# Norms, constants and the last blocks taken by halves in a three-block kernel on one core

## What is computed

```python
def third_block(x, c, ...):
    mod = jax.nn.silu(c) @ w_ada + b_ada
    shift1, scale1, gate1, shift2, scale2, gate2 = jnp.split(mod, 6, axis=-1)
    h = rms_norm_3(x, norm1_pre) * (1.0 + scale1) + shift1
    z = h @ w_in
    y_a = spatial_gating(z[..., : 2 * D_A], ...)
    y_b = multiscale_pool(z[..., 2 * D_A:], ...)
    mix = jnp.concatenate([y_a, y_b], axis=-1) @ w_out
    x = x + gate1 * rms_norm_3(mix, norm1_post)
    h = rms_norm_3(x, norm2_pre) * (1.0 + scale2) + shift2
    f = jnp.square(jax.nn.relu(h @ w_fc1)) @ w_fc2
    x = x + gate2 * rms_norm_3(f, norm2_post)
    return x
```

## Time and profile before

| | |
|---|---|
| median of 3 runs | 3709.75 us (3709.17 to 3716.92) |
| profiled execution | 3709.14 us, span 3707.4 us |
| mean granted TensorE clock | 0.965 |
| busy: PE | 3542.8 us (96%) |
| busy: DVE, ACT, POOL | 43%, 27%, 34% |
| DMA | 239.79 MB, mean 65 GB/s |

### The profile page before, as it was taken

One profiled execution on the slowest core, in us unless ns is written; L12 is line 12 of the kernel. 1 busy time (PEld: TensorE's weight loads), 2 busy tenths in 40 slices (PEclk: granted clock), 3 DMA queues, 4 the chain that ended last, 5 costly groups with the idle time before them and its releaser, 6 DMA issues.

```text
span 3707.4 us, 39394 instructions
## 1 busy us (share of the span) xinstructions
PE 3542.8 (96%) x17066; PEld 2843.6 (77%) x17066; DVE 1600.2 (43%) x1611; ACT 999.8 (27%) x1422; POOL 1253.5 (34%) x628
## 2 busy tenths in 40 slices
PE   8999999999999999989999999999998889999997
PEld 6888888888888787545787777877877678888885
DVE  4643443433335383546545445444535341222224
ACT  5423221111113211545332212212322332222221
POOL 3113245444445131002223334434524343333332
PEclk9999999999999999959999999999999899999998
DMA  2112222222223121100211222221311111111113
GB/s 104 46 57 80 91 71 86 89 90 80 83 83 114 35 69 37 39 3 1 74 46 51 87 84 63 90 86 62 95 36 34 63 54 46 49 49 49 49 49 114
DMA packets 87416, 239.79 MB, mean 65 GB/s; under 512 B 13110, under 2 KB 20038, under 8 KB 87116
## 3 DMA queue, kind: packets, MB, share of 16 engines
q1 hardware_dynamic: 87244, 237.28, 19.8%
HBM read 219.27 MB, written 17.97 MB: 64 GB/s over the span
## 4 chain that ended last, share of the span: by engine, by line
PE 91%; DVE 5%; ACT 2%; POOL 1%; issue 0%; DMA 0%; SPq 0%; DVEq 0%; ACTq 0%
PE ps L570 27%; PE ps L571 27%; PE ps L573 26%; PE ps L877 1%; PE ps L907 1%; PE ps L927 1%; PE ps L942 1%; PE ps L705 1%; PE ps L625 1%; PE ps L989 1%; PE ps L973 1%; DVE T L1713 1%; DVE T L1738 0%; DVE P L2113 0%; DVE T L1716 0%
## 5 line engine op out<-in xcount | busy, mean ns | idle before, releaser
L2425 POOL TENSOR_TENSOR wlo<-raw,whi 128x1024 fp32r<-128x1024 f32 (+3 forms) x368 | 698.6, 1898 | 1713.6 <-ACT whi L1155 1713.2
L570 PE MATMUL ps<-HH,whi 128*128 128x512 f32 (+2 forms) x2816 | 1119.6, 398 | 46.8 <-DVE HL L1729 13.7
L571 PE MATMUL ps<-HL,whi 128*128 128x512 f32 (+2 forms) x2816 | 1106.7, 393 | 0.0
L573 PE MATMUL ps<-HH,wlo 128*128 128x512 f32 (+2 forms) x2816 | 874.8, 392 | 0.0
L1155 ACT ACTIVATE whi<-raw 128x1024 fp32r<-128x1024 f32 (+3 forms) x368 | 310.9, 845 | 1722.6 <-PE ps L573 1548.2
L570 PEld LDWEIGHTS ps<-HH,whi 128*128 128x128 f32 (+2 forms) x2816 | 531.7, 189 | 168.8 <-DVE HL L1729 18.3
L570 PE MATMUL ps<-GH,whi 128*128 128x512 f32 x1536 | 609.7, 397 | 15.7 <-POOL wlo L2425 12.5
L573 PEld LDWEIGHTS ps<-HH,wlo 128*128 128x128 f32 (+2 forms) x2816 | 530.6, 188 | 116.7 <-issue 0.6
L571 PEld LDWEIGHTS ps<-HL,whi 128*128 128x128 f32 (+2 forms) x2816 | 531.8, 189 | 112.9 <-issue 2.0
L571 PE MATMUL ps<-GL,whi 128*128 128x512 f32 x1536 | 601.6, 392 | 0.0
L573 PE MATMUL ps<-GH,wlo 128*128 128x512 f32 x1536 | 477.1, 392 | 0.0
(11 more groups left out here) (335 smaller groups left out, 2930.7 us busy)
## 6 DMA issues: line engine op xcount, KB each, us to landing
raw<-in_w_up SPq DMA_DIRECT2D x76, 512.0 KB, 3.4
raw<-in_w_in SPq DMA_DIRECT2D x70, 512.0 KB, 3.3
raw<-in_w_fc SPq DMA_DIRECT2D x64, 512.0 KB, 3.3
raw<-in_w_down SPq DMA_DIRECT2D x104, 256.0 KB, 2.7
raw<-in_w_ada SPq DMA_DIRECT2D x48, 512.0 KB, 3.4
raw<-in_w_fc SPq DMA_DIRECT2D x64, 256.0 KB, 2.7
X<-in_xT SPq DMA_DIRECT2D x16, 512.0 KB, 7.3
raw<-in_w_out SPq DMA_DIRECT2D x16, 512.0 KB, 3.3
```

Of the source, the lines that this page charges most:

```text
L570: e.matmul(o_[0:m, half(hf)], whi_[:, k, :], hi[k0 + k][:, half(hf)], start=first, stop=False)
L571: e.matmul(o_[0:m, half(hf)], whi_[:, k, :], lo[k0 + k][:, half(hf)], start=False, stop=False)
L573: i = e.matmul(o_[0:m, half(hf)], wlo_[:, k, :], hi[k0 + k][:, half(hf)], start=False, stop=last)
L2425: e.tensor_tensor(wlo_of(name), raw_of(name), whi_of(name).bitcast(F), SUB).then_inc(*po.inc("lo " + name))
```

## The change

Five parts:

1. **Spreads.** The spread of the norms n2, n3, nl, n4 and n5 goes into misc in the middle of a product, instead of into a PSUM buffer after it. ScalarE's copy to RT stands ahead of the next weight split. The conv norm's sums (nl) come one product later, its spread within the one after.
2. **Constants.** ADA_AT loses items 0, 1, 2 and gains 51, 63, 75. ROW_AT is redrawn. Before: every item from 3 to 61 except those that 4 divides. After: 2, 3, 4, 13, then in each group three of the four up items (14, 15, 16; 26, 27, 28; ...) and seven of the eight down items (19 to 25; 31 to 37; ...). Before the group's last hidden tile, ScalarE and GpSimd now split the next down products' weights.
3. **The mixer's end.** wo36 and wo37 are taken by halves of the tokens: both for the first half, then both for the second. Norm, mixn, x6, hh6, hl6 and squares go by halves.
4. **Three up products by blocks.** fa1_0, fa1_1 and fa1_2 go along together: for each half and block, the three matmuls of each. A third high-half buffer WX serves fa1_1.
5. **The tail.** fa2_7_6 and fa2_7_7 by halves; nf, xo, out and the output DMAs by halves; the gain is multiplied into X by ScalarE ahead.

```diff
-ADA_AT = sorted([0, 1, 2] + [n for n in range(4, 88) if (n - 4) % 12 in (0, 1, 2, 5, 7, 9)] + [15, 27, 39])
-ROW_AT = [n for n in range(3, 62) if n % 4]
+ADA_AT = sorted([n for n in range(4, 88) if (n - 4) % 12 in (0, 1, 2, 5, 7, 9)] + [15, 27, 39, 51, 63, 75])
+ROW_AT = [n for n in range(2, 62) if n < 5 or n == 13 or 14 <= n < 53 and (n - 14) % 12 < 3
+          or n >= 18 and (n - 18) % 12 in range(1, 8)]
...
         def tensor(e):
+            def halves(names, hi, lo, toks, nk, k0=0, between=None, along=False):
+                parts = []
+                for hf in range(2):
+                    order = [(n, k) for k in range(nk) for n in range(len(names))] if along else [(n, k) for n in range(len(names)) for k in range(nk)]
+                    for n, k in order:
+                        if n == len(parts):
+                            parts.append((take(names[n]),) + weights(names[n], nk))
+                            q.wait_ge(*po("lo " + names[n]))
+                        o_, whi_, wlo_ = parts[n]
+                        if between:
+                            between(names[n], hf, k)
+                        for tok in toks(k0 + k, hf):
+                            q.wait_ge(*tok)
+                        e.matmul(o_[:, half(hf)], whi_[:, k, :], hi[k0 + k][:, half(hf)], start=k == 0, stop=False)
+                        e.matmul(o_[:, half(hf)], whi_[:, k, :], lo[k0 + k][:, half(hf)], start=False, stop=False)
+                        i = e.matmul(o_[:, half(hf)], wlo_[:, k, :], hi[k0 + k][:, half(hf)], start=False, stop=k == nk - 1)
...
-            job("gv0", hhs, hls, h3, 8)
-            spread("n3 sp", two, dv("n3 r12"))
+            job("gv0", hhs, hls, h3, 8, between=lambda k: k == 6 and spread_misc("n3 sp", two, dv("n3 r12"), dv("n3 s2")))
...
-            job("zv1", hhs, hls, h5, 8)
-            spread("n5 sp", two, dv("n5 r12"))
+            job("zv1", hhs, hls, h5, 8, between=lambda k: k == 5 and spread_misc("n5 sp", two, dv("n5 r12"), dv("b43")))
...
-            sums("nm", dv("nm acc7"))
-            spread("nm sp", one, dv("nm r1"))
-            mlp("fa1_", "fa2_", [4] * 8, lambda k: [dv(f"hl6 {k}")], "nx", dv("nx acc7"), joint=True)
-            sums("nf", dv("nf acc7"))
-            spread("nf sp", one, dv("nf r1"))
+            def mix_norm(name, hf, k):
+                if (name, hf, k) == ("wo36", 1, 4):
+                    sums_half("nm", 0, 512, dv("nm acc7 h0"))
+                elif (name, hf, k) == ("wo37", 1, 1):
+                    spread_half("nm", 0, misc, dv("nm r1 h0"))
+            halves(["wo36", "wo37"], hhs, hls, lambda k, hf: [y3[k]], 8, between=mix_norm)
+            def next_norm(name, hf, k):
+                if (name, hf, k) == ("fa1_0", 0, 3):
+                    sums_half("nm", 1, 512, dv("nm acc7 h1"), ac("nm sd h0"))
+                elif (name, hf, k) == ("fa1_0", 0, 7):
+                    spread_half("nm", 1, misc, dv("nm r1 h1"))
+                elif (name, hf, k) == ("fa1_0", 1, 4):
+                    sums_half("nx", 0, 0, dv("nx acc7 h0"), dv("mixn 7 0"))
+            halves(["fa1_0", "fa1_1", "fa1_2"], hhs, hls, lambda k, hf: [dv(f"hl6 {k} {hf}")], 8, between=next_norm, along=True)
+            sums_half("nx", 1, 512, dv("nx acc7 h1"), dv("mixn 7 1"))
+            spread_half("nx", 0, misc, dv("nx r1 h0"))
+            spread_half("nx", 1, misc, dv("nx r1 h1"))
...
         def scalar(e):
+            mixed(6, 0)
+            mixed(7, 0)
+            root_half("nm", 0, 512)
+            mixed(6, 1)
+            behind("wo36")
+            highs(widx["fa1_1"])
+            for hf in range(2):
+                h = half(hf)
+                for k in range(8):
+                    high(f"hh6 {k} {hf}", X[:, k, h], HH[:, k, h], po(f"x6 {k} {hf}"), pe("wo37"), scale=gains[:, 16 + k:17 + k])
+                    if (k, hf) == (1, 0):
+                        mixed(7, 1)
+                        highs(widx["fa1_2"])
...
+            root_half("nx", 1, 512)
+            for hf in range(2):
+                q.wait_ge(*pe(f"nx sp{hf}"))
+                e.activation(RT[:, half(hf)], misc[:, half(hf)], ACT.Copy).then_inc(*ac.inc("nx rt" if hf else "nx rt0"))
...
         def gpsimd(e):
+                    if g and j == SIZES2[g] - 1:
+                        for j_ in range(3 if g == 1 else 1):
+                            behind(f"fdn{g - 1}_{j_}")
                     low(f"fuplo{m}", T[CT[m][1]][:], GH[:, sl, :], GL[:, sl, :], ac(f"fuphi{m}"))
```

More of the change, by code:

```diff
@@ L856, in tensor @@
                 for m in range(3):
-                    job(f"{name}{m}", hhs, hls, h3, 8)
+                    job(f"{name}{m}", hhs, hls, h3, 8, between=None if n != 15 else lambda k: k == 5 and spread_misc("nl sp", one, dv("nl r1")))
                     turn_now()
@@ L1073, in tensor @@
                         sums("n4", dv("n4 acc7"))
-                    job(f"fupb{m}", hhs, hls, lambda k: [dv(f"hl4 {k}")], 8)
-                    if m == 0:
-                        spread("n4 sp", one, dv("n4 r1"))
+                    job(f"fupb{m}", hhs, hls, lambda k: [dv(f"hl4 {k}")], 8,
+                        between=None if m else lambda k: k == 5 and spread_misc("n4 sp", one, dv("n4 r1")))
                 else:
@@ L1369, in mlp @@
                         f = 4 * g + j
+                        if f == 1 and norm:
+                            to_rt(norm, *rt_free)
                         behind(f"{up}{f}")
@@ L1687, in scalar @@
                     q.wait_ge(*po("y3l3"))
-                square("nm", m, ps[slot[f"wo3{m}"]][:], *([dv("uu3")] if m == 0 else []))
-                e.activation(MIX[:, m, :], ps[slot[f"wo3{m}"]][:], ACT.Copy, scale=gains[:, 8 + m:9 + m]).then_inc(*ac.inc(f"mix{m}", f"free wo3{m}"))
-            root("nm", 1024)
-            done = 0
-            for k in range(8):
-                high(f"hh6 {k}", X[:, k, :], HH[:, k, :], at_x6(k), pe("wo37"), scale=gains[:, 16 + k:17 + k])
-                if k in (0, 1, 2, 4, 6):
-                    square("nx", done, X[:, done, :], *([pe("nm sp")] if k == 0 else []))
-                    done += 1
```

300 lines of the change are left out of this document (201 added, 99 removed).

## The result

The changed kernel takes 3618.5 us in the median of four runs (3615.57 to 3619.77), against 3711.26 us before (3709.17 to 3716.92, four runs). The ratio is 0.9747, with a 95% interval from 0.973 to 0.9763: faster, by 92.8 us. The profiled execution has a span of 3616.3 us (before 3707.4), and its mean granted clock is 0.975 (before 0.965).

What follows compares the result with a forecast made beforehand. TensorE bounds the kernel, 91% of the span; the change can only remove standstill or low clock. Gains of 26, 33, 18 and 5 us sum to 82, giving 3627, median 3628 us; range 3603 to 3656, chance 0.83.

Steps and rivals of the forecast that it cites:

- Spreads inside products: Five norms' spreads moved into the middle of products: TensorE's gaps and clock dips there go; gain 26 us, bounds 0 to 26.
- the nine microseconds of the conv norm: Conv norm: the 4.81 us wait for its sums and a 4.2 us clock dip go, 9.0 us.
- Constants moved: Second MLP's constants moved, weights split earlier: 14.5 of 47.5 us stay; gain 33 us, bounds 10 and 47.5.
- the rival of a binding supply: Each of 28 down products with a constant waits 0.8 us, so that region gains 10 us: 3651; chance 0.13.
- The slower rival: The constants' reduction falls behind in each of 28 rows, slower from 3.7 us a row on: 3773; chance 0.03.
- The mixer's end: Last output products to the fourth up product, by halves: 53.6 us against 71.3; gain 18 us, bounds 0 and 30.
- The first block comes 1.4 us later: Mixer's end: HH may be written only when both last output products are through, delaying the first block 1.4 us.
- The third product's 3.8 us: Mixer's end, first block: the third product waits about 3.8 us for fa1_2's high and low halves.
- fa1_3's 4.2 us: Mixer's end: fa1_3's high half stands behind both RT copies on ScalarE, costing 4.2 us.
- The rival of the halves that lock each other out: Mixer's blocks: VectorE and GpSimd block each other, 3.5 us a half block against TensorE's 2.04: 3648; chance 0.12.
- The tail: Last product to the span's end, by halves: 26 us instead of 31.3; gain 5 us, bounds 0 and 9.
- half of 0.07: Rival: 14.5 us left with the constants and 12 of 15.3 us at the mixer's end vanish: 3602; chance 0.07.

Runs made afterwards that it cites:

- experiment 12: The changed kernel measured once more, unaltered: 3615.67 us, ratio 0.974.
- experiment 5: The changed kernel with the seven rows of constants of each group taken one down product earlier: 3637.2 us, ratio 0.9796.
- experiment 9: The changed kernel with the high half of fa1_3 ahead of the last root on ScalarE: 3613.76 us, ratio 0.9734.
- experiment 10: The changed kernel with experiments 8 and 9 joined and GpSimd's three additions of squares in each half moved to VectorE: 3619.35 us, ratio 0.9749.
- experiments 8: The changed kernel with x6 0 ahead of fa1_1's low half, fa1_2's low half one block earlier, its high half ahead of hh6 0: 3618.93 us, ratio 0.9749.

## Why the prediction was right, step by step

**Spreads inside products: right, mechanism and size.** No gap is left at the five places. The forecast's 4.1, 4.3, 2.6 and 6.2 us stand against 4.4 and 6.3 us measured when undone, and for the two in the middle against gaps of 2.60 and 2.56 that came back. The conv norm was never undone by itself. In the comparison of the two kernels its stage with n3's gave 18.4 us where the forecast had 13.3. The difference is 5.1 us, which is what the dip at 1202 us differs by (13.65 us long before, 3.41 after, at half clock), and this dip is the one that comes and goes in experiment 12. So the nine microseconds of the conv norm agree, but they are read off and not shown by a run.

**Constants moved: the mechanism right, the term mis-sized.** "Gain 33 us" was 41.4. The waits of before were 36.0 us, as read. Two numbers in the step were off. First, the dips: "47.5 us in all" had 11.5 us for the clock and 4 us of dips left over, so 7.5 net, and it is 12.6. I took a granted clock of windows at two group starts and a mean of 2.0; the records have the clock at half for 6.83 us at each of the four and for 10.24 at the first. Second, what is late next: I had 10.5 us of stillness left, and it was 7.2. The place was right (ahead of up products, and 0.3 at the group starts), and the reason too: experiment 5 took the buffer's wait away and the gaps with it. But I had charged 2 us to each of three groups and 1 us to shared loads; it was 1.05, 2.25 and 1.09, and nothing. At the first, short group it was 1.46 and not 2.1. At the down products with a constant there was no wait at all, so the rival of a binding supply (3651) had nothing in it.

**The slower rival.** The reduction did not fall behind in 28 rows. But its mechanism exists one product away: experiment 5 has 3.73 us at each group's first down product, just the 3.7 us a row that I named as deciding, in four rows and not in 28. What spares the others is GpSimd: at those it has no hidden tile ahead of the row.

**The mixer's end: right size, one step wrong inside it.** 17.0 us against 18. "The first block comes 1.4 us later" failed: I had left out that the low halves of fa1_0 and fa1_1 stand ahead of x6 0 on GpSimd, and it was 4.20 us. The third product's 3.8 us was 1.74, since it waits for a fixed time on GpSimd whatever came before; the two sum to 5.9 against my 5.2. The turn cost 2.00 us and not 1.4. fa1_3's 4.2 us was 4.14, for the reason named, as experiment 9 shows.

**The rival of the halves that lock each other out.** Here I argued with the wrong evidence. hl6 halves have a mean of 1.29 us and x6 halves 1.62; my 1.1 and 1.47 were too low. The groups of VectorE by form in the changed kernel, between 2876 and 2919 us:

```profile
L1834 DVE SCALAR_TENSOR_TENSOR HL<-X,gains,HH 128x512 fp32r<-128x512 f32 x16 | 20.6, 1293 | 7.7 <-ACT HH L1290 7.7
L1831 DVE TENSOR_TENSOR T<-T,T 128x512 f32<-128x512 f32 x9 | 11.6, 1288 | 1.3 <-POOL T L2586 1.3
L1831 DVE TENSOR_TENSOR MIX<-MIX,ps 128x512 f32<-128x512 f32 x13 | 8.6, 674 | 0.0
```

VectorE is busy for 38.0 of these 43 us (the busy times of the rows overlap and add up to more). The mechanism is real, at 2.94 us a half block (experiment 10) and not 3.5. It did not set the time of the changed kernel, as its gaps lie elsewhere; it took the gain of experiments 8 and 10. The Trainium skill, SBUF — State Buffer, "Who interferes with whom", says that a VectorE instruction with two SBUF inputs contends with a GpSimd one that reads SBUF. This trace agrees: 1.76 us beside x6 and 0.68 without for two inputs from SBUF, 0.67 us in either case with one from PSUM. The words "fully blocks", which the prediction leans on, stand there of VectorE's two-port modes; the rows bear them out for this addition too, which ended 0.56 us after the x6 beside it.

**The tail: right mechanism, 23.1 us where 26 was forecast.** The last square, sum and root took 3.6 us and not 5.5, the rest 0.8 and 0.3 less. From 31.3 us that is 8.2 us less. The last row of the table has 6.8, since from the fourth up product to the last product's end it takes 1.4 us more than before. That is not the clock, which is at half for about 6 us there in both kernels. Most of it is the first half's sums and spread, which now lie inside the last product: 0.81 us from 3589.56 on and 0.35 us from 3591.86 on.

**The rest.** That the total fits as well as its parts is in part luck. 5.1 us of the gain are the dip at 1202 us, which was the short one in the changed kernel's profile and the long one before, and the start and the attention took back 5.4 us by the same kind of chance. The spans of one kernel differ by 9.4 us, a tenth of the gain. The chances that the prediction puts into its range, 0.62, 0.13, 0.12 and half of 0.07, add up to 0.90 and not to 0.83. Left open: what decides between the long and the short dip, and the conv norm's share.

## What to carry to other kernels

Compare two kernels at events that both have, and not by their totals: here chance, most of it in the clock, moved a total by 3 to 9 us, which hid an 8 us gain and made a 7.4 us loss look like 15.2. A helper's work (a constant's row, a weight's split) costs nothing at most places and 3.7 us at the wrong one; to find the wrong ones, read for each place what stands ahead of it in the queue of every engine that it passes, GpSimd's above all. Before work is moved between VectorE and GpSimd, count the inputs from SBUF: where VectorE had two and GpSimd read there as well, the engines took turns, and the sum of their times was the bound.

## What the hardware showed that I had not expected

After one and the same gap of 1.8 us near 1202 us the granted clock was at 1.2 GHz for 3.41 us in one execution of the changed kernel and for 13.65 us in another, 5 us of difference. A dip priced from one trace has that much chance in it.

An addition of 512 columns from SBUF to SBUF on VectorE took 1.76 us beside GpSimd and 0.68 without it: by the rows it is not slowed in proportion but held until GpSimd's instruction is nearly through, and it ended 0.56 us after the x6 beside it.
